# Eight projection tiles on x times the norm's weights, scaled behind the product, in a one-core decoder block

## The reference, cut to what matters

```
xn   = x * rsqrt(mean(x*x over channels) + 1e-6) * norm_mix_g
proj = xn @ w_in                  # 1024 x 6144
b_gate, c_gate, h, p = proj[...]  # 1024 columns each; g_a and g_b are the rest
conv = w[0]*z[t-2] + w[1]*z[t-1] + w[2]*z[t]      with z = c_gate * h
y_a  = (b_gate * conv) @ w_conv_out
pool = (sum of the last win p) / min(t+1, win) - p    # win = 2, 4, 8, 16 by quarter of the channels
y_b  = (pool @ pool_w * pool_scale) @ w_pool_out
```

## Time and profile before

| | |
|---|---|
| median of 3 runs | 1723.2 us (1722.98 to 1723.83) |
| the profiled execution | 1723.17 us, of which 1721.4 us lie between its first and last instruction (the span) |
| PE busy | 98% of the span |
| VectorE busy | 75% |
| ScalarE busy | 39% |
| mean granted TensorE clock | 0.994 of full speed |

### The profile page before, as it was taken

One profiled execution on the slowest core, in us unless ns is written; L12 is line 12 of the kernel. 1 busy time (PEld: TensorE's weight loads), 2 busy tenths in 40 slices (PEclk: granted clock), 3 DMA queues, 4 the chain that ended last, 5 costly groups with the idle time before them and its releaser, 6 DMA issues.

```text
span 1721.4 us, 27467 instructions
## 1 busy us (share of the span) xinstructions
PE 1680.8 (98%) x9671; PEld 1571.0 (91%) x9671; DVE 1285.7 (75%) x2280; ACT 670.4 (39%) x872; POOL 289.5 (17%) x267
## 2 busy tenths in 40 slices
PE   5999999999799999999999999999999999999997
PEld 4888788888588999999999999999999999999997
DVE  6555533334457899998999998677788888888885
ACT  4222443333333333334656656333333333333332
POOL 0000000000000101003222222441223332333230
PEclk9999999999899999999999999999999999999998
DMA  4222332222222566659888899998899999999991
GB/s 167 94 94 97 109 111 97 88 95 98 85 74 85 193 213 224 225 197 335 306 323 325 325 331 331 376 376 297 301 338 377 364 377 376 356 387 359 363 319 60
DMA packets 121871, 415.29 MB, mean 241 GB/s; under 512 B 13664, under 2 KB 16736, under 8 KB 120160
## 3 DMA queue, kind: packets, MB, share of 16 engines
q1 hardware_dynamic: 75456, 234.16, 38.0%
q0 software_dynamic: 36864, 134.23, 21.7%
q10 hardware_dynamic: 9504, 46.40, 6.7%
HBM read 366.25 MB, written 48.50 MB: 241 GB/s over the span
## 4 chain that ended last, share of the span: by engine, by line
PE 86%; DVE 10%; issue 3%; ACT 1%; DMA 0%; DVEq 0%; SPq 0%; ACTq 0%
PE bank L707 16%; PE bank L709 16%; PE bank L708 16%; PE bank L840 11%; PE bank L841 11%; PE bank L842 11%; PE bank L824 4%; DVE w_lo L884 1%; DVE rows L1158 1%; PE bank L771 1%; DVE less L1075 1%; DVE scratch L924 1%; DVE top_i L1082 1%; DVE top_i L1074 1%; DVE xn_lo L918 1%
## 5 line engine op out<-in xcount | busy, mean ns | idle before, releaser
L884 DVE TENSOR_TENSOR w_lo<-w_raw,w_hi 128x1024 fp32r<-128x1024 f32 x348 | 424.9, 1221 | 223.8 <-ACT w_hi L496 223.7
L707 PE MATMUL bank<-xn_hi,w_hi 128*128 128x384 f32 (+1 forms) x1536 | 550.5, 358 | 7.8 <-DVE xn_lo L918 6.5
L496 ACT ACTIVATE w_hi<-w_raw 128x1024 fp32r<-128x1024 f32 x348 | 367.7, 1057 | 485.4 <-PE bank L842 325.3
L709 PE MATMUL bank<-xn_hi,w_lo 128*128 128x384 f32 (+1 forms) x1536 | 543.9, 354 | 0.0
L708 PE MATMUL bank<-xn_lo,w_hi 128*128 128x384 f32 (+1 forms) x1536 | 543.6, 354 | 0.0
L840 PE MATMUL bank<-a_hi,w_hi 128*128 128x384 f32 x1024 | 348.4, 340 | 0.0
L841 PE MATMUL bank<-a_lo,w_hi 128*128 128x384 f32 x1024 | 347.8, 340 | 0.0
L842 PE MATMUL bank<-a_hi,w_lo 128*128 128x384 f32 x1024 | 347.8, 340 | 0.0
L459 POOL DMA_INDIRECT rows<-u_rows,expert x128 | 146.0, 1140 | 1077.4 <-DVE expert L1183 576.4
L707 PEld LDWEIGHTS bank<-xn_hi,w_hi 128*128 128x128 f32 x1536 | 289.1, 188 | 36.4 <-issue 9.1
L709 PEld LDWEIGHTS bank<-xn_hi,w_lo 128*128 128x128 f32 x1536 | 289.3, 188 | 20.9
(11 more groups left out here) (172 smaller groups left out, 1244.4 us busy)
## 6 DMA issues: line engine op xcount, KB each, us to landing
w_raw<-u SPq DMA_DIRECT2D x128, 512.0 KB, 4.4
w_raw<-v SPq DMA_DIRECT2D x128, 512.0 KB, 6.2
g_dram<-g_sb ACTq DMA_DIRECT2D x12, 2048.0 KB, 9.6
g_in<-g_dram SPq DMA_DIRECT2D x84, 256.0 KB, 8.0
act_dram<-act_out ACTq DMA_DIRECT2D x54, 384.0 KB, 4.8
act_in<-act_dram SPq DMA_DIRECT2D x54, 384.0 KB, 7.0
w_raw<-w_in SPq DMA_DIRECT2D x32, 512.0 KB, 3.2
w_raw<-gate SPq DMA_DIRECT2D x32, 512.0 KB, 3.2
```

The source lines that it names most:

```text
L496: act.activation(w_hi[:, slot, :], w_raw[:, slot, :], ACT.Copy).then_inc(hi_done, 1)
L707: pe.matmul(out, hi, act_hi[:, k, tokens], start=k == 0, stop=False)
L709: last = pe.matmul(out, lo, act_hi[:, k, tokens], start=False, stop=k == NB - 1)
L884: dve.tensor_tensor(w_lo[:, slot, :], w_raw[:, slot, :], w_hi[:, slot, :].bitcast(F32), ALU.subtract).then_inc(lo_done, 1)
```

## The change

For the first two groups (tiles 0 to 7) PE multiplies `xg`, which is x times the norm's weights without the factor of the token. `xg_hi` is made by ScalarE straight from x, `xg_lo` by VectorE; the two use the places of `u_hi`, `u_lo`, `mix_hi` and `mix_lo` that are written only later, so the rows call them by those names. The squares, their sum and the spreading now come after: ScalarE squares once `xg_hi` and weight tile 1 are done, PE sums behind tile 1 and spreads behind tile 2. The results of the eight tiles are scaled afterwards on VectorE: p by r, c_gate by r squared (it then covers h as well), the convolution by r once more before it meets b_gate. The true xn, which the groups from the third on need, is made on VectorE and ScalarE between the work of groups 0 and 1. x is loaded in turn by SyncE and ScalarE, `params` goes first on ScalarE's queue, weight tile 0 second on SyncE's. PE starts with 16 products of the all-ones tile by itself, into bank 6, which nobody reads.

```diff
 X_PARTS = 4
+RAW_GROUPS = 2
+WARM_PRODUCTS = 16
...
         mix_lo = front("mix_lo", [P, NB, T], F32R)
+        xg_hi = [u_hi[:, 2 + j, :] if j < NB - 2 else mix_hi[:, 2 + j - (NB - 2), :] for j in range(NB)]
+        xg_lo = [u_lo[:, 2 + j, :] if j < NB - 2 else mix_lo[:, 2 + j - (NB - 2), :] for j in range(NB)]
...
+        def load_x(engine, k):
+
+            blocks = slice(k * NB // X_PARTS, (k + 1) * NB // X_PARTS)
+            engine.dma_start(h_t[:, blocks, :], x_t[:, blocks, :]).then_inc(x_loaded[k], 16)
...
-            for k in range(X_PARTS):
-                blocks = slice(k * NB // X_PARTS, (k + 1) * NB // X_PARTS)
-                sp.dma_start(h_t[:, blocks, :], x_t[:, blocks, :]).then_inc(x_loaded[k], 16)
-            sp.dma_start(params[:], params_d).then_inc(params_loaded, 16)
-            for b in range(SLOTS):
+            load_x(sp, 0)
+            load_raw(w_in_d, 0, 0, 0)
+            load_x(sp, 2)
+            for b in range(1, SLOTS):
                 load_raw(w_in_d, b, b, b)
...
+            act.dma_start(params[:], params_d).then_inc(params_loaded, 16)
+            load_x(act, 1)
+            load_x(act, 3)
             act.wait_ge(consts, 1)
             load_root_table(1)
+            act.wait_ge(params_loaded, 16)
             for j in range(NB):
                 if j % (NB // X_PARTS) == 0:
                     act.wait_ge(x_loaded[j * X_PARTS // NB], 16)
+                act.activation(xg_hi[j], h_t[:, j, :], ACT.Copy,
+                               scale=params[:, COL_G_MIX + j:COL_G_MIX + j + 1]).then_inc(xg_h, 1)
+                if j == NB // X_PARTS - 1:
+                    split_weight(0, 0, 1)
+            split_weight(1, 1, 1)
+            for j in range(NB):
                 act.activation(squares[:, j, :], h_t[:, j, :], ACT.Square).then_inc(squared, 1)
-            split_weight(0, 0, 1)
+            split_weight(2, 2, 1)
             root(1)
-            split_weight(1, 1, 1)
-            norm_hi(0)
-            split_weight(2, 2, 1)
             split_weight(3, 3, 1)
...
-
-            with act.Fori(0, NB) as i:
+            act.wait_ge(spread, 1)
+            act.activation(row_stat[:], bank[5][:], ACT.Copy).then_inc(spread_copied, 1)
+
+            def norm_block(j):
+                act.wait_ge(xn_f, j + 1)
+                act.activation(xn_hi[:, j, :], scratch[:, j % 2, :], ACT.Copy).then_inc(xn_h, 1)
+
+            def pool_hi(i):
+                act.wait_ge(pf_ready, i + 1)
...
+            def u_high(i):
+                act.wait_ge(uf_ready, i + 1)
...
+            for i in range(RAW_GROUPS):
+                split_weight(SLOTS * i + 4, 0, i + 2)
+                pool_hi(i)
+                for j in range(4 * i, 2 + 6 * i):
+                    norm_block(j)
+                for b in range(1, SLOTS):
+                    split_weight(SLOTS * i + 4 + b, b, i + 2)
+                u_high(i)
+                if i == 0:
+                    norm_block(2)
+                    norm_block(3)
+
+            with act.Fori(RAW_GROUPS, NB) as i:
                 act.wait_ge(job_done, SLOTS * i + 1)
                 act.activation(p_pad[:, PAD:], bank[0][:], ACT.Copy).then_inc(p_copied, 1)
                 split_weight(SLOTS * i + 4, 0, i + 2)
...
                     out = bank[b][:, tokens]
-                    pe.matmul(out, hi, act_hi[:, k, tokens], start=k == 0, stop=False)
-                    pe.matmul(out, hi, act_lo[:, k, tokens], start=False, stop=False)
-                    last = pe.matmul(out, lo, act_hi[:, k, tokens], start=False, stop=k == NB - 1)
+                    x_hi, x_lo = (x[k] if isinstance(x, list) else x[:, k, tokens] for x in (act_hi, act_lo))
+                    pe.matmul(out, hi, x_hi, start=k == 0, stop=False)
+                    pe.matmul(out, hi, x_lo, start=False, stop=False)
+                    last = pe.matmul(out, lo, x_hi, start=False, stop=k == NB - 1)
...
-            pe.wait_ge(consts, 7)
-            pe.wait_ge(added, 1)
-            sum_squares(4, squares[:, 0, :], 0)
-            spread_inverse(5, 1)
-
-            with pe.Fori(0, NB) as i:
+            pe.wait_ge(consts, 1)
+            for _ in range(WARM_PRODUCTS):
+                pe.matmul(bank[6][:, 0:P], ones[:], ones[:], start=True, stop=True)
+            for n in range(SLOTS * RAW_GROUPS):
+                tile_product(n, n % SLOTS, n // SLOTS + 1, xg_hi, xg_lo, xg_l if n == 0 else None)
+                if n == 1:
+                    pe.wait_ge(added, 1)
+                    sum_squares(4, squares[:, 0, :], 0)
+                if n == 2:
+                    spread_inverse(5, 1)
+
+            with pe.Fori(RAW_GROUPS, NB) as i:
                 for b in range(SLOTS):
                     tile_product(SLOTS * i + b, b, i + 1, xn_hi, xn_lo, xn_l if b == 0 else None)
...
+
+            def norm_full(base, gain_col, j):
+                if j >= 2:
+                    dve.wait_ge(xn_l, base + j - 1)
+                dve.scalar_tensor_tensor(scratch[:, j % 2, :], h_t[:, j, :],
+                                         params[:, gain_col + j:gain_col + j + 1], bank[5][:],
+                                         ALU.mult, ALU.mult).then_inc(xn_f, 1)
+
+            def norm_low(base, j):
+                dve.wait_ge(xn_h, base + j + 1)
+                dve.tensor_tensor(xn_lo[:, j, :], scratch[:, j % 2, :], xn_hi[:, j, :].bitcast(F32),
+                                  ALU.subtract).then_inc(xn_l, 1)
 
...
+            dve.wait_ge(params_loaded, 16)
+            for j in range(NB):
+                dve.wait_ge(xg_h, j + 1)
+                dve.scalar_tensor_tensor(xg_lo[j], h_t[:, j, :], params[:, COL_G_MIX + j:COL_G_MIX + j + 1],
+                                         xg_hi[j].bitcast(F32), ALU.mult, ALU.subtract).then_inc(xg_l, 1)
+                if j == NB // X_PARTS - 1:
+                    split_weight(0, 0)
+            split_weight(1, 1)
...
-            split_weight(0, 0)
-            dve.wait_ge(params_loaded, 16)
+            split_weight(2, 2)
             dve.wait_ge(consts, 7)
+            dve.tensor_copy(ident_r[:], ident[:]).then_inc(ident_ready, 1)
             dve.wait_ge(summed, 1)
             inverse_rms(bank[4], 1)
-            norm_apply(0, COL_G_MIX)
...
+            split_weight(3, 3)
+            dve.wait_ge(spread_copied, 1)
+
+
+            def pool_block(i, window):
...
                                   ALU.subtract).then_inc(pf_ready, 1)
-                split_weight(SLOTS * i + 4, 0)
+
...
+                if raw:
+                    chain.wait()
+                    chain.did(dve.tensor_tensor(conv[:, 0, :], conv[:, 0, :], row_stat[:], ALU.mult))
                 dve.wait_ge(job_done, SLOTS * i + 4)
                 chain.wait()
                 dve.tensor_tensor(u_f[:], bank[3][:], conv[:, 0, :], ALU.mult).then_inc(uf_ready, 1)
+
+            def conv_low(i):
...
-            for g, window in enumerate(WINDOWS):
-                with dve.Fori(2 * g, 2 * g + 2) as i:
-                    chain.enter(i - 2 * g, 4 + (window.bit_length() - 1) + 2)
...
+            def scaled_p(i):
+
+                dve.wait_ge(job_done, SLOTS * i + 1)
+                dve.tensor_tensor(p_pad[:, PAD:], bank[0][:], row_stat[:], ALU.mult).then_inc(p_copied, 1)
+
+            def scaled_c(i):
+
+                dve.wait_ge(job_done, SLOTS * i + 2)
+                dve.tensor_tensor(c_sb[:], bank[1][:], mixed_f[:], ALU.mult).then_inc(c_copied, 1)
+
+
+            scaled_p(0)
+            chain.did(dve.tensor_tensor(mixed_f[:], row_stat[:], row_stat[:], ALU.mult))
+            chain.wait()
+            scaled_c(0)
+            pool_block(0, WINDOWS[0])
+            split_weight(4, 0)
+            norm_full(0, COL_G_MIX, 0)
+            norm_full(0, COL_G_MIX, 1)
+            pool_low(0)
+            norm_low(0, 0)
+            norm_low(0, 1)
+            split_weight(5, 1)
+            conv_block(0, raw=True)
+            norm_full(0, COL_G_MIX, 2)
+            norm_full(0, COL_G_MIX, 3)
+            conv_low(0)
+            norm_low(0, 2)
+            norm_low(0, 3)
+
+            scaled_p(1)
+            scaled_c(1)
+            pool_block(1, WINDOWS[0])
+            split_weight(8, 0)
+            norm_full(0, COL_G_MIX, 4)
+            norm_full(0, COL_G_MIX, 5)
+            pool_low(1)
+            norm_low(0, 4)
+            norm_full(0, COL_G_MIX, 6)
+            norm_low(0, 5)
+            norm_full(0, COL_G_MIX, 7)
+            norm_low(0, 6)
+            norm_low(0, 7)
+            split_weight(9, 1)
+            conv_block(1, raw=True)
+            conv_low(1)
+
+            for g, window in enumerate(WINDOWS[1:]):
+                with dve.Fori(2 * g + RAW_GROUPS, 2 * g + 2 + RAW_GROUPS) as i:
+                    chain.enter(i - (2 * g + RAW_GROUPS), 4 + (window.bit_length() - 1) + 2)
```

More of the change, by code:

```diff
@@ L323, in build @@
         h_ready = sem("h_ready")
+        xg_h, xg_l = sem("xg_h"), sem("xg_l")
         xn_f = sem("xn_f")
@@ L998, in in_block @@
```

(14 more changed lines are left out.)

42 lines of the change are left out of this document (16 added, 26 removed).

## The result

The changed kernel takes 1713.91 us (median of 5 runs, 1712.92 to 1715.90), the kernel before 1722.98 in the same comparison. The ratio is 0.9948 with a 95% interval of 0.9934 to 0.9963: 9.1 us faster, forecast 10.4. The profiled execution took 1713.85, its span is 1712.1.

A forecast was written before the change was run, and what follows sets the result against it. PE was taken as the bound, busy 1680.8 of 1721.4 us, its longest wait 12.1 us at the start. Tile 9 at 64.1 instead of 74.47 wins 10.4 us: 1723.17 - 10.4 = 1712.8, range 1710.9 to 1717.0.

The forecast's parts named there:

- The loads: At the start: tile 0's weights land at 8.8 us, between third (8.2) and fourth transfer; at worst fifth, 10.9.
- The doubt about the second queue: At the start: by the skill's rule strictly, nothing lands sooner through a second queue; the order alone could help.
- VectorE's terms: Before tile 9: scalar_tensor_tensors 0.75 us each, additions 0.8 each; VectorE's work from 36.0 to tile 9's low part 27.7.
- the waits of 0.4 and 0.9 us at tiles 4 and 9: PE waits 0.4 us for VectorE's scalings before tile 4 and 0.9 us before tile 9.
- the sum: All forecast terms added up as they stand, without any rival: 1712.8 us, chance 0.50.
- PE's term: In the projections: each tile takes PE 5.44 us, 0.227 us a matmul.
- Rival A: At tile 0: the clock has fallen again in PE's pause; 1.7 us more, 1714.5 us; chance 0.22.
- the likeliest case: The whole kernel with the terms as they stand and no rival: 1712.8 us, chance 0.50.
- B: At the loads: two queues bring nothing, weights land fifth at 10.9; 2.1 us more, 1714.9 us; chance 0.13.
- C: In groups 0 and 1: VectorE is the bound, ScalarE's answers uncovered; 4.8 us more, 1717.6 us; chance 0.05.
- D: In tiles 0 to 3: waits keep PE at 1.2 GHz, slower than before, about 1732 us; chance 0.03.
- Half a microsecond at the start is half a microsecond at the end: Whole kernel: time won on PE near the start moves everything behind it by the same amount, unless a later wait takes it.

The follow-up runs named there:

- experiment 2: Changed kernel with all four parts of x on SyncE's queue, weight tile 0 second, params alone on ScalarE's: 1711.09 us, ratio 0.9931.
- experiment 1: Changed kernel with 34 instead of 16 constant products at the start: 1711.50 us; with none: 1714.16 us.
- Experiment 5: Changed kernel with nine constant products ahead of the second norm's sum of squares and seven before its spreading: 1712.62 us, ratio 0.9938.
- experiment 4: Operand regions behind params moved by padding: changed kernel 1701.91 us (32 bytes), 1703.38 (64), 1696.93 (96), 1702.74 (224 and 128); kernel before, 96 bytes, 1708.60.
- experiment 6: Changed kernel with 96 bytes padding, x on SyncE's queue: 1694.97 us; last kernel adds 26 start products, products at second and third norms: 1693.67.

## Why the prediction was right, and where its steps were off

The mechanism was right: PE's stream starts early, VectorE's chain of squares runs beside it, and the gain at tile 9 carries through the kernel. Tile 9 stands at 64.39 against a forecast of 64.1, the gain there is 10.2 against 10.4, and 9.3 are left at the end of the span. That tile 9 is right to 0.3 us is in part luck, since several terms were off and cancel, as follows.

*The loads.* 8.08 instead of 8.8, so the weights landed at about the place of a third transfer (8.2), and tile 0 began 0.7 us sooner than forecast. That was inside the bounds. The doubt about the second queue was more than right: it is a loss of 1.2 us at tile 0 (experiment 2). The Trainium skill (DMA: Bandwidth & Descriptors, "Issuing engines are not separate DMA queues") says that transfers run on the same DMA engines and interleave, whichever engine started them. The runs agree: with parts of x on the second queue the weights on the first came at 8.08, without them they were there by 6.85.

*VectorE's terms were too dear.* Six scalar_tensor_tensors step by 0.66 us instead of 0.75 (14.28 - 10.31 for six), the additions by 0.77 instead of 0.80, and from tile 4's low part at 36.2 to tile 9's at 61.5 VectorE needs 25.3 us, not 28.1. So the waits of 0.4 and 0.9 us at tiles 4 and 9 did not come. Back to back, one instruction starts before the last has ended, and the sum should have taken steps, not durations.

*PE's term was too cheap.* The forecast took 5.44 us a tile from tiles on xn and counted it for tiles on the places of u and mix: seven tiles at the high clock, 0.18 more each, are 1.3 us. The rows to see it by were in the trace of the kernel before, in the gates and w_out (of the 32 gate tiles only half read xn, the others u and mix). From tile 4 to tile 9 the two errors cancel: 28.1 us forecast, with PE waiting for VectorE, 28.06 measured, with longer tiles and no wait. Ahead of tile 4 the sooner weights (0.7) and the shorter waits on VectorE, net of the longer tiles (0.6), make up for the low clock in tile 0 (1.6), all but 0.3 us. The sum was better than its terms.

*Rival A came true, and the likeliest case was not the one that happened in this profile.* The clock was low until 14.2, and tile 1 began at 17.70 where 16.8 was forecast without A; tile 2 came at 24.13, ahead of A's 24.9 to 25.9, and the time of 1713.91 lies between the sum's 1712.8 and A's 1714.5. It cost 1.6 us in tile 0 (experiment 1) in this profile; in three others with the same products it was absent. So A looks less like a case against the sum than like a draw made at each run. That much of the scatter of 3 us comes from such draws is not shown by traces, since one execution of each kernel has one, but the mean granted clock of the five runs fits it: 0.993 for the fastest (1712.92), 0.990 for the slowest (1715.90), and in order between. The Trainium skill (TensorE: Matmul & The Clock Gate, "HAM oscillation — how this bites in real kernels") describes waits between bursts of matmuls that put the engine back to the low clock. The profile after agrees (0.43 us in tile 0 behind 4.2 us of waiting); of the other profiles, pauses of 3.4 us left the clock high in one and not in another, so here the pause by itself does not decide.

*B, C and D* did not occur: weights at 8.1, no PE wait on VectorE between the start of tile 0 and tile 9, the high clock from 14.2 to the second norm.

*"Half a microsecond at the start is half a microsecond at the end"* failed by 0.8 us. The step had no place for the clock at the second norm: the same pause of 3.06 us that left it high before (1.05 us for the sum) left it low after (1.86). Experiment 5 filled that pause and got 1.05 back. That the missing 0.8 us is there is shown by the two profiles. It is again a draw: of twelve profiles with this same pause six had 1.05, as the kernel with one queue, and five 1.86 or 1.87 (experiment 5). That another execution of the changed kernel itself would draw the other way is likely, not shown.

## What to carry to other kernels

When a norm's factor can be taken out of a product, the product need not wait for it: here 6.5 us by the medians, and the scalings on VectorE made PE wait nowhere. Load in the order of use on one queue; a second queue let in what was needed later. And compare the step of the same matmul between stages: a stage that steps by 2 or 3% more at the same clock may only need its operand moved; 96 bytes, with nothing else changed, took 15.2 us off the kernel before, more than the whole change did. When the clock at a pause is a draw, take a gain of 1 or 2 us from one profile for what it is, one draw.

## What the runs showed of the hardware

The rate of a stream of matmuls depends on where in the memory its moving operand stands: 0.227, 0.233 or 0.234 us for 512 columns, 0.1735 or 0.1767 for 384, with nothing else changed (experiment 4). The rule behind it is open.

The column of the granted clock is no sure witness at the start of an execution. In the kernel before it prints 1.00 for 0 to 27 us, while the matmuls of 512 columns step by 0.43 us until 26.8, the step of the low clock. In the changed kernel it follows in tile 0, but it also prints 1.00 until 3.8, while the products step by 0.213 us (experiment 1). In both the wrong reading ends where the clock first changes:

```profile
12.00:14.00 2.00, 2.00 (x6) 1.56 (x5) 2.00 (x4) 2.00 (x3) 0.00 (x0) 0.50 1.03 406
```

At the start the step is the better witness.

The clock can also fall while PE is busy: at the third norm of the last kernel of experiment 6 it went from 1.00 to 0.50 within an unbroken stream of small matmuls, and in experiment 5's profile tile 0 began at 10.51 with steps of 0.23, fell to 0.43 at 11.5 and came back at 14.9, without a wait between.

The same pause can leave the clock high or low: behind 3.06 us at the second norm eight one-column records took 1.05 us in six profiles and 1.86 or 1.87 in five.
